# Second block's q, k, v and u products: joined 512-column matmuls, and two of eight weight remainders on GpSimd

## The reference, cut to what matters

```python
h = rms_norm_2(x, norm1_w[l], RMS_EPS)
z = h @ w_in[l]                       # 2048 columns in, q, k, v, u and gates out
y_ssm = s5_mixer(z[..., :o_q], ...)   # u: 8 blocks of 128 columns
y_attn = diff_attention(z[..., o_q:o_k], z[..., o_k:o_v], z[..., o_v:o_gs], ...)   # q, k, v of 8 heads
```

## Time and profile before

| | |
|---|---|
| median of 3 runs | 2418.33 us (2418.19 to 2419.38) |
| profiled execution, its own time | 2421.73 us |
| its span | 2420.0 us |
| TensorE busy / VectorE busy / ScalarE busy / GpSimd busy | 99% / 71% / 50% / 22% |
| mean granted TensorE clock | 0.999 |

### The profile page before, as it was taken

One profiled execution on the slowest core, in us unless ns is written; L12 is line 12 of the kernel. 1 busy time (PEld: TensorE's weight loads), 2 busy tenths in 40 slices (PEclk: granted clock), 3 DMA queues, 4 the chain that ended last, 5 costly groups with the idle time before them and its releaser, 6 DMA issues.

```text
span 2420.0 us, 45086 instructions
## 1 busy us (share of the span) xinstructions
PE 2400.7 (99%) x15288; PEld 2170.0 (90%) x15288; DVE 1714.1 (71%) x2644; ACT 1218.7 (50%) x1834; POOL 526.8 (22%) x1002
## 2 busy tenths in 40 slices
PE   9999999999999999999999999999999999999999
PEld 7878888998999999999999999998888888888888
DVE  8877776668888887678888876666555555555556
ACT  6444454455666665556665444444444444444442
POOL 2210032246767773210021221111000000000000
PEclk9999999999999999999999999999999999999999
DMA  7756576666666665565567777756777777777774
GB/s 253 238 177 199 187 227 202 197 195 197 192 205 210 198 197 183 184 203 188 161 196 248 257 224 232 232 193 186 199 191 191 191 191 190 190 190 192 190 190 151
DMA packets 257244, 485.07 MB, mean 200 GB/s; under 512 B 23704, under 2 KB 171876, under 8 KB 256880
## 3 DMA queue, kind: packets, MB, share of 16 engines
q1 hardware_dynamic: 216208, 415.66, 56.5%
q10 hardware_dynamic: 29632, 35.30, 4.6%
q0 software_dynamic: 11296, 32.68, 4.5%
HBM read 455.20 MB, written 31.08 MB: 201 GB/s over the span
## 4 chain that ended last, share of the span: by engine, by line
PE 82%; DVE 7%; DMA 4%; issue 3%; ACT 2%; POOL 1%; ACTq 0%; DVEq 0%; SPq 0%; POOLq 0%
PE z_ps L2233 12%; PE z_ps L2221 9%; PE z_ps L2222 9%; PE z_ps L2223 9%; PE z_ps L2649 7%; PE z_ps L2650 7%; PE z_ps L2655 7%; PE z_ps L2234 6%; DVE w_lo L1404 3%; DMA arena<-na_pad_d 1%; ACT w_hi L752 1%; DMA na_pad_d<-na_one_d 1%; DMA na_bias_d<-arena 1%; PE o_ps L2276 1%; PE s_ps L2258 1%
## 5 line engine op out<-in xcount | busy, mean ns | idle before, releaser
L1404 DVE TENSOR_TENSOR w_lo<-w_raw,w_hi 128x1024 fp32r<-128x1024 f32 x518 | 641.1, 1267 | 215.9 <-ACT w_hi L752 213.9
L752 ACT ACTIVATE w_hi<-w_raw 128x1024 fp32r<-128x1024 f32 x518 | 528.5, 1050 | 229.6 <-PE z_ps L2234 115.7
L2089 DVE TENSOR_TENSOR w_lo<-w_raw,w_hi 128x1024 fp32r<-128x1024 f32 x262 | 320.8, 1226 | 300.5 <-ACT w_hi L1244 300.5
L2233 PE MATMUL z_ps<-x_both,w_hi 128*128 128x512 f32 x1432 | 513.3, 401 | 0.7 <-DVE w_lo L1397 0.5
L1244 ACT ACTIVATE w_hi<-w_raw 128x1024 fp32r<-128x1024 f32 x262 | 277.9, 1061 | 415.3 <-PE z_ps L2655 267.8
L2234 PE MATMUL z_ps<-x_both,w_lo 128*128 128x256 f32 x1432 | 401.2, 280 | 0.0
L2221 PE MATMUL z_ps<-x_both,w_hi 128*128 128x256 f32 x1376 | 397.8, 289 | 1.1 <-DVEq L1941 0.8
L2223 PE MATMUL z_ps<-x_both,w_lo 128*128 128x256 f32 x1376 | 389.3, 283 | 0.0
L2222 PE MATMUL z_ps<-x_both,w_hi 128*128 128x256 f32 x1376 | 389.2, 283 | 0.0
L2233 PEld LDWEIGHTS z_ps<-x_both,w_hi 128*128 128x128 f32 x1432 | 269.6, 188 | 63.6 <-DVE w_lo L1397 0.8
L2649 PE MATMUL z_ps<-w_hi,x_both 128*128 128x512 f32 x704 | 275.0, 391 | 0.0
(11 more groups left out here) (474 smaller groups left out, 4186.9 us busy)
## 6 DMA issues: line engine op xcount, KB each, us to landing
w_raw<-in_w SPq DMA_DIRECT2D x624, 512.0 KB, 4.3
w_raw<-in_w SPq DMA_DIRECT2D x160, 256.0 KB, 3.3
w_raw<-in_w SPq DMA_DIRECT2D x80, 384.0 KB, 4.9
w_raw<-in_w SPq DMA_DIRECT2D x80, 128.0 KB, 3.0
tab_d<-arena ACTq DMA_DIRECT2D x32, 256.0 KB, 3.0
res<-tab_d POOLq DMA_DIRECT2D x16, 384.0 KB, 5.6
arena<-tab_d POOLq DMA_DIRECT2D x16, 384.0 KB, 6.1
tab_d<-arena ACTq DMA_DIRECT2D x32, 128.0 KB, 2.8
```

Source lines behind the costliest of these rows:

```text
L752: act.activation(w_hi[:, n % RING, :], w_raw[:, n % RING, :], ACT.Copy).then_inc(w_hi_ready, 1)
L1404: dve.tensor_tensor(w_lo[:, n % RING, :], w_raw[:, n % RING, :], w_hi[:, n % RING, :].bitcast(F32), ALU.subtract).then_inc(w_lo_ready, 1)
L2089: dve.tensor_tensor(w_lo[:, k % RING, :], w_raw[:, k % RING, :], w_hi[:, k % RING, :].bitcast(F32), ALU.subtract).then_inc(w_lo_ready, 1)
L2233: pe.matmul(z[:], wh, both[:, :, kt, :], start=(first and kt == kts[0]), stop=False)
```

## The change

Jobs 0 to 3 of the eight head periods take the joined form (`job4`, `job4_around`). On VectorE `evac2` becomes a sum of the halves and a product (the semaphore `z_free` now goes up after the sum and `z_added` after the product, and those who read q, k or v wait for `z_added`), and `evac_u` a strided sum and a product in place. In periods 1 to 7 the remainders of chunks 3 and 7 are computed by GpSimd (`split_second`), while VectorE computes chunks 2 and 6; VectorE then waits for GpSimd and raises `w_lo_ready` for it. GpSimd's two splits of a period stand in its queue ahead of the bias loads of the next head, and those of period 7 ahead of the first tables and inputs. `rpb_pad`'s memset moves within GpSimd's first instructions and shares a semaphore.

```diff
+            def split_second(p, c):                                    # GpSimd
+                n = 2 * c + 1
+                pool.wait_ge(w_hi_ready, 8 * p + n + 1)
+                pool.tensor_tensor(w_lo[:, n % RING, :], w_raw[:, n % RING, :], w_hi[:, n % RING, :].bitcast(F32),
+                                   ALU.subtract).then_inc(pool_lo, 1)
             with pool.Fori(2, N_DH) as i:
+                split_second(P_QKV + i - 1, 1)
+                split_second(P_QKV + i - 1, 3)
                 attention(i)
+            split_second(P_QKV + N_DH - 1, 1)
+            split_second(P_QKV + N_DH - 1, 3)
             pool.wait_ge(x2_stored, 16)
             load_pair(0)
...
-                act.wait_ge(z_free, taken(p, 1))                       # ScalarE, attn_3
+                act.wait_ge(z_added, added2(i, 1))
...
-            def evac2(dst, p, c, ring=2):                              # VectorE
-                job_done(p, c)
-                dve.tensor_tensor(dst, z_ps[c % ring][:, 0, :], rstd[:], ALU.mult).then_inc(z_free, 1)
+            def evac2(dst, p, c):
+                halves_sum(dst, p, c)
+                dve.tensor_tensor(dst, dst, rstd[:], ALU.mult).then_inc(z_added, 1)
             def evac_u(p):
                 job_done(p, 3)
-                dve.tensor_tensor(zz.rearrange("p (i k) -> p k i", i=STEP),
-                                  z_ps[3][:, 0, :].rearrange("p (k i) -> p k i", i=STEP),
-                                  rstd[:].rearrange("p (k i) -> p k i", i=STEP), ALU.mult).then_inc(z_free, 1)
+                dve.tensor_reduce(zz.rearrange("p (i k) -> p k i", i=STEP),
+                                  z_ps[3][:].rearrange("p a (k i) -> p k i a", i=STEP), AX_X, ALU.add).then_inc(z_free, 1)
+                dve.wait_ge(z_free, taken(p, 3))
+                dve.tensor_tensor(zz.rearrange("p (i k) -> p i k", i=STEP), zz.rearrange("p (i k) -> p i k", i=STEP),
+                                  rstd[:].rearrange("p (k i) -> p i k", i=STEP), ALU.mult).then_inc(u_ready, 1)
+            def split_both(p, i, c):
+                split_lo(p, c, (0,))
+                dve.wait_ge(pool_lo, 2 * i - 1 + c // 2)
+                dve.wait_ge(w_lo_ready, 8 * p + 2 * c + 1)
+                dve.sem_inc(w_lo_ready, 1)
             def head_2(i, prev=True, prev2=True, prev3=True, x2=False):
-                split_lo(p, 1)
+                split_both(p, i, 1)
...
-                split_lo(p, 3)
+                split_both(p, i, 3)
...
+            def job4(p, c, wait_kt=None):                              # TensorE
+                pe.wait_ge(z_free, taken(p, c - 4))
+                job_joined(z_ps[c], p, c, x_both, wait_kt)
+            def job4_around(p, c, i, prev2):
+                pe.wait_ge(z_free, taken(p, c - 4))
+                for s in range(2):
+                    chunk_joined(z_ps[c], p, 2 * c + s, range(CH * s, CH * (s + 1)), x_both, s == 0,
+                                 s == 1).then_inc(w_free, 1)
+                    if s == 0 and prev2:
+                        output_sums(i)
             def head_2(i, prev=True, prev2=True, sums=False):
-                job2(p, 0, x_hi, x_lo, ..., 4)
+                job4(p, 0, ...)
-                job2(p, 1, x_hi, x_lo, ring=4)
+                job4(p, 1)
-                job2_around(p, 2, i, prev2)
-                job2(p, 3, x_hi, x_lo, ring=4)
+                job4_around(p, 2, i, prev2)
+                job4(p, 3)
```

More of the change, by code:

```diff
@@ L283, in build @@
         y_lo_ready = sem("y_lo_ready")
-        pad_zeroed = sem("pad_zeroed")
+        pool_lo = sem("pool_lo")
         pad_filled = sem("pad_filled")
@@ L421, in added, with added2 @@
             return 4 * p + c + 1 if l == 0 else 4 * HEADS + 2 * (p - PERIODS_LAYER) + c + 1
+        def added2(i, c):
+            return 4 * HEADS + 2 * HEADS + 2 + 3 * i + c + 1
         def ffn_base(g):
@@ L530, in _ @@
             pool.memset(msq_sum[:], 0.0).then_inc(msq_summed, 1)
-            pool.memset(rpb_pad, 0.0).then_inc(pad_zeroed, 1)
             pool.wait_ge(ones_ident_ready, 2)
@@ L534, in _ @@
                                pattern=[[-1, P]], channel_multiplier=1).then_inc(ones_ident_ready, 1)
+            pool.memset(rpb_pad, 0.0).then_inc(ones_ident_ready, 1)
             def sum_squares(l, n, two):
@@ L545, in _ @@
             pool.tensor_tensor(x_sq[0], x_sq[0], x_sq[1], ALU.add).then_inc(xsq_step, 1)
-            pool.wait_ge(pad_zeroed, 1)
+            pool.wait_ge(ones_ident_ready, 4)
             c0 = GRID_W - 1 - (RPB_COLS - 1) // 2
@@ L1834, in head_2 @@
                     evac_u(p - 1)
-                    dve.wait_ge(z_free, taken(p - 1, 3))
-                    dve.sem_inc(u_ready, 1)
                 attn_0(i, prev, prev3, x2)
@@ L1839, in head_2 @@
                 attn_1(i, prev, prev2)
-                evac2(qk[:, 0, :], p, 0, 4)
-                split_lo(p, 3)
+                evac2(qk[:, 0, :], p, 0)
+                split_both(p, i, 3)
                 attn_2(i, prev)
@@ L1844, in head_2 @@
                 attn_inverse(i, prev2)
-                evac2(qk[:, 1, :], p, 1, 4)
+                evac2(qk[:, 1, :], p, 1)
                 attn_3(i, prev)
@@ L1849, in head_2 @@
                     dve.wait_ge(scores2_done, i)
-                evac2(v2_t, p, 2, 4)
+                evac2(v2_t, p, 2)
                 attn_4(i, prev2)
@@ L1872, in _ @@
             dve.wait_ge(norm_step, N0 + 8)
-            evac2(qk[:, 0, :], P_QKV, 0, 4)
+            evac2(qk[:, 0, :], P_QKV, 0)
             split_lo(P_QKV, 3)
-            evac2(qk[:, 1, :], P_QKV, 1, 4)
+            evac2(qk[:, 1, :], P_QKV, 1)
             dve.wait_ge(param_landed, 32)
@@ L1894, in _ @@
             split_lo(P_QKV, 4)
-            evac2(v2_t, P_QKV, 2, 4)
+            evac2(v2_t, P_QKV, 2)
             to_x2(range(5, 10))
@@ L2009, in _ @@
             evac_u(P_GATE - 1)
-            dve.wait_ge(z_free, taken(P_GATE - 1, 3))
-            dve.sem_inc(u_ready, 1)
             dve.wait_ge(x2_stored, 16)
@@ L2059, in x3_block @@
                 dve.tensor_tensor(res[:, n, :], zb(p, c), res[:, n, :], ALU.add).then_inc(z_added, 1)
-                dve.wait_ge(z_added, added(HEADS, 0) + 2 * HEADS + n + 2)
+                dve.wait_ge(z_added, added2(N_DH, -1) + n + 1)
                 dve.tensor_tensor(res[:, n, :], z_ps[c % 2][:, 1, :], res[:, n, :], ALU.add).then_inc(z_free, 1)
@@ L2480, in scores2 @@
                 pe.wait_ge(qk_n_ready, i)
-                pe.wait_ge(z_free, taken(P_QKV + i - 1, 2))
+                pe.wait_ge(z_added, added2(i - 1, 2))
                 if prev2:
@@ L2520, in head_2 @@
                 p = P_QKV + i
-                job2(p, 0, x_hi, x_lo, (lambda kt: pe.wait_ge(x_lo_ready, DEPTH * KT + kt + 1)) if sums else None, 4)
+                job4(p, 0, (lambda kt: pe.wait_ge(x_lo_ready, DEPTH * KT + kt + 1)) if sums else None)
                 if sums:
```

## The result

The changed kernel takes 2457.09 us (median of 4 runs, 2455.79 to 2459.58), the kernel before in the same comparison 2418.86 (4 runs, 2418.19 to 2420.19): a ratio of 1.0159, 95% interval 1.0141 to 1.0176. The forecast was 2454.

What follows compares the result with a forecast made beforehand. The prediction took the closed round of VectorE and ScalarE (27.12 us a period) as the bound. Periods 1 and 2 (+4, +3.5), 3 to 7 (+27) and after the heads (+1.5) gave +36 us on 2418.33: 2454, range 2434 to 2466.

Steps and rivals of the forecast that it cites:

- The bound: Head periods: VectorE and ScalarE form a closed round of 27.12 us, slower than TensorE's own 26.91 us a period.
- q, k and v: VectorE's evacuations: a sum of halves added to each product, +2.0 us a period after some 0.17 goes into a wait.
- u: VectorE's evacuation of u: one strided instruction becomes a strided sum and product, +0.7 us a period (+0.4 to +0.8).
- GpSimd's first split: Chunk 3: GpSimd takes 2.4 us, so VectorE goes on later, ahead of u and the norm: +1.4 us a period.
- GpSimd's second split: Chunk 7: VectorE saves a 1.1 us subtraction but is blocked 2.2 us beside GpSimd: +1.1 us a period net.
- The Trainium skill's rule: VectorE instructions with two SBUF inputs and GpSimd instructions reading SBUF exclude each other; the later one is fully blocked.
- The sum: A head period: VectorE's additions total +5.2 us, a round of 32.3 us; TensorE's period grows by 5.4 us.
- First periods: Head periods 1 and 2, with TensorE's lead still being used up: +4 us and +3.5 us.
- After the heads: First gate period: VectorE arrives later against TensorE by u's 0.7 us and the lost lead, +1.5 us.
- The loads behind GpSimd's splits: Table and input loads issued after period 7's splits: they cost nothing, with 10 us left for landing.
- The clock's rival: TensorE's clock falls after each `scores2` wait, losing 1.7 us, or GpSimd is slower: period 1.2 us longer, 2462 to 2466; 12%.
- TensorE as the bound: Head periods: VectorE only trails TensorE, so joined matmuls give 6.4 us, 0.8 a period: 2412 us; chance 5%.

Runs made afterwards that it cites:

- Experiment 1: Changed kernel with VectorE computing all eight remainders of a period again, matmuls still joined: 2442.27 us, ratio 1.0079.
- experiment 2: Kernel before with only GpSimd's two splits a period and VectorE's waits for them added, matmuls at 256 columns: 2440.18 us, ratio 1.0077.
- experiment 6: Changed kernel with 22 extra matmuls of 256 columns in TensorE's idle time ahead of `scores2`, periods 2 to 7: 2460.58 us, ratio 1.0159.
- Experiment 8: Kernel before's 256-column matmuls with GpSimd's two splits, chunk 7's held back, chunk 3's wait behind `y_lo`, mean ahead of u: 2419.87 us, ratio 0.9995.
- experiment 4: Changed kernel with VectorE's wait for GpSimd's split of chunk 3 moved behind u, the mean and `y_lo`: 2453.27 us, ratio 1.0123.
- experiment 5: Changed kernel reordered: chunk 7's split held back, wait for chunk 3's split behind `y_lo`, mean of the norm ahead of u: 2420.56 us, ratio 0.9999.
- experiment 7: Reordered kernel (experiment 5) with q, k and v of head 0 unjoined as in the kernel before: 2421.49 us, ratio 0.9996.
- experiment 3: Changed kernel with GpSimd's split of chunk 7 held until VectorE has finished chunk 6, VectorE waiting for it later: 2442.8 us, ratio 1.0086.

## Why the prediction was right, point by point

- **The bound.** Right. It rested on 0.21 us between two beats. Experiment 1 gave VectorE more work and TensorE less, experiment 2 touched only VectorE and GpSimd, and both times the period grew on 27.12 by what VectorE's timeline accounts for, while experiment 6 gave TensorE more work and its full clock and nothing moved. Experiment 8 is the other side: with VectorE's round shorter than 26.91, the period is 26.91.
- **q, k and v**, +2.0: measured 3 x 0.72 - 0.26 = 1.9.
- **u**, +0.7, between 0.4 and 0.8: measured 0.5. The stride cost the product 0.2 (0.61 against 0.42) and the sum nothing (0.69 against 0.68).
- **GpSimd's first split**, +1.4: measured 1.6. Its length, 2.46 us, was put at 2.4; the way back to VectorE takes 0.39 us and not 0.1.
- **GpSimd's second split**, +1.1: measured 1.4. The block is 2.2 us, as said, and fell on the squaring; the subtraction given away saves 0.8 and not 1.1. The Trainium skill's rule ("SBUF — State Buffer", section "Who interferes with whom") agrees with the instances shown here: in experiment 4 u's product (two inputs in SBUF) is held, 2.10 against 0.61, u's sum from PSUM is not. The page restricts its exemption for one SBUF input to instructions outside the 2-port modes; L1784, 0.29 us where an instruction of that size from PSUM takes 0.41, was held with a single one. Its speed and the hold fit such a mode; no run here shows the mode itself.
- **The sum**: 5.2 forecast, 5.37 measured, on TensorE's period 5.4 forecast and 5.58 measured (32.49 - 26.91). Two terms were too large by 0.3 together, two too small by 0.5, so that the sum is nearer than its terms.
- **First periods**, +4 and +3.5: `turn2` of period 1 is 4.7 us later than before (1094.23 against 1089.52), of which 0.4 stems from the first block, and that of period 2 another 3.2. The prediction's own terms for period 2, 5.4 - 1.5 - 0.8, make 3.1 and not the 3.5 that it added; that 7.5 came out for both periods together is partly luck.
- **After the heads**, +1.5: `turn2` of period 7 is 35.8 us later, the span 37.9 longer, so 2.1. The first gate period's wait for VectorE's evacuation has grown from 0.47 to 1.49 us, and one of 0.36 (at 1288.74) is new. The loads behind GpSimd's splits cost nothing visible: they are issued by 1281.76, and the state-space matmuls at 1295.26 start without a wait.
- **The clock's rival.** Its mechanism came true: behind each wait of 2.8 us the lower level. Its price didn't, and the reason given against it (the waits that follow hide it) is what experiment 6 shows. But the margin was thin. A clock of 0.89 over 32.4 us is 3.6 us lost in one period, 0.95 is 1.6 in the next, and the prediction had 1.7. In the first kind of period TensorE has no wait left ahead of `turn2`, in the second 1.44 us. For the same reason joined K tiles didn't start 0.347 us apart throughout, as it said, but 0.64 for some 5 us of such a period.
- **TensorE as the bound.** Experiments 5, 7 and 8 reach that case by placing the work, and the price of 6.4 us was too high: 0.58 us a period, of which experiment 5 gives back 2.2 of 2.9 us in the first periods. No version measured was faster than the kernel before by what can be told apart.

Open stays why some joined K tiles of the reordered kernel take 0.353 us and others 0.347, and whether the single waits behind the heads in experiments 5 and 7 belong to the order of work or to the execution; a kernel's runs on that chip spread over some 7 us (2417.5 to 2424.3 in experiment 5), more than what is looked for. Much of that arises ahead of the heads: their first product starts between 1035.00 us (experiment 5) and 1042.45 us (experiment 4) in the ten profiled executions, behind code that differs at most in GpSimd's first instructions. This is why the periods, and not the times, tell the last microseconds apart here.

## What to carry to other kernels

Before handing work from VectorE to GpSimd, look for two things: who in VectorE's order waits for it soon, and at which instructions VectorE is while GpSimd reads SBUF. Instructions with at most one operand from SBUF kept their lengths here, except the one that scales or clamps from SBUF to SBUF (TENSOR_SCALAR). Placed without regard to that, 2.3 us of subtractions given away made VectorE's round 3.0 us longer; placed with regard to it they cost nothing (experiment 8), and gained nothing either, since TensorE's pace was then the bound. And where two engines' beats are within 1%, as here, the busy shares don't name the bound: look for the engine whose waits form a closed round. In this kernel work on the other one (wider matmuls, a better clock) was worth nothing until the round was shorter.

## What the runs showed of the hardware that was not expected

- A TENSOR_SCALAR of 128x256 from SBUF to SBUF, with one tensor operand, is held until GpSimd's subtraction ends, like one with two: 2.47 us beside it against 0.29 without it. A TENSOR_REDUCE with one operand from SBUF is not (1.13 us for four either way, experiment 3).
- The record of GpSimd's instruction includes the time it is held: 3.40 us when it starts under VectorE's subtraction of 1.22 us, 2.38 to 2.50 when it starts as VectorE's ends.
- From the end of GpSimd's instruction to VectorE's next, with a wait and a semaphore raised between them, 0.39 us passed (1197.54 to 1197.93).
